# Decay tables of a head pair: VectorE's small operations given to ScalarE, two sums kept on VectorE behind the sum into v

## The reference, cut to what matters

```
idx = jnp.arange(CHUNK, dtype=jnp.float32)
diff = idx[:, None] - idx[None, :]
allowed = diff >= (1.0 if strict else 0.0)
decay_in = jnp.where(allowed[None], jnp.exp(jnp.where(allowed, diff, 0.0)[None] * log_g[:, None, None]), 0.0)
decay_q = jnp.exp((idx + 1.0)[None, :] * log_g[:, None])[None, :, :, None]
decay_k = jnp.exp((CHUNK - 1.0 - idx)[None, :] * log_g[:, None])[None, :, :, None]
...
    scores = jnp.einsum('bhqd,bhkd->bhqk', qc, kc) * decay_in
    inner = jnp.einsum('bhqk,bhke->bhqe', scores, vc)
    cross = jnp.einsum('bhqd,bhde->bhqe', qc * decay_q, state)
```

## Time and profile before

| | |
|---|---|
| median of 3 runs | 2592.87 us (2592.4 to 2595.53) |
| span of the profiled execution | 2588.9 us; the profile gives no device time of its own, so the 4.0 us to the median are what lies around the span |
| PE busy | 2518.4 us of the span (97%) |
| DVE busy | 1859.0 us (72%) |
| ACT busy | 1166.0 us (45%) |
| POOL busy | 1722.0 us (67%) |
| mean granted TensorE clock | 0.993 |
| the four pairs of the first sequence | about 57 to 583 us of the span |
| the four pairs of the second sequence | about 1343 to 1855 us |

### The profile page before, as it was taken

The page is one execution under the profiler, slowest core; times in us unless marked ns, Lnnn a source line. Parts: engine busy times, 40 slices in busy tenths (PEclk is TensorE's granted clock), DMA queues, the critical chain, the costliest instruction groups (busy, mean ns, idle before and its releaser), DMA issues.

```text
span 2588.9 us, 34797 instructions
## 1 busy us (share of the span) xinstructions
PE 2518.4 (97%) x12684; PEld 2104.9 (81%) x12684; DVE 1859.0 (72%) x2230; ACT 1166.0 (45%) x1770; POOL 1722.0 (67%) x1165
## 2 busy tenths in 40 slices
PE   6999999989999999999999999999999999999998
PEld 3888888878778888878888888888877888888886
DVE  4989898977886666765868898988678555556434
ACT  5433333235654554555633333333455554555443
POOL 1677777756287777645656868686655777775545
PEclk9999999999999999999999999999999999999998
DMA  9124242446144445497631514141541323325764
GB/s 330 41 87 132 84 135 84 151 154 216 41 155 159 155 163 176 149 346 232 187 124 41 161 58 160 59 149 47 190 131 41 126 78 122 106 86 194 207 193 146
DMA packets 296008, 362.14 MB, mean 140 GB/s; under 512 B 17312, under 2 KB 178464, under 8 KB 295840
## 3 DMA queue, kind: packets, MB, share of 16 engines
q1 hardware_dynamic: 292960, 349.44, 41.9%
q10 hardware_dynamic: 2880, 10.49, 1.1%
HBM read 284.36 MB, written 75.50 MB: 139 GB/s over the span
## 4 chain that ended last, share of the span: by engine, by line
PE 66%; DVE 15%; POOL 8%; issue 5%; DMA 4%; ACT 3%; SPq 1%; POOLq 0%; DVEq 0%; ACTq 0%
PE ps L1097 27%; PE ps L1263 14%; PE ps L1527 8%; PE ps L1158 5%; POOL f_w L2187 4%; PE ps L1368 3%; PE ps L1478 2%; DVE late_rows L2670 2%; DMA f_ring<-in_w_in 1%; PE ps L1195 1%; POOL f_ring L2195 1%; DVE merged_t L2970 1%; PE ps L1546 1%; DVE bufB L2820 1%; POOL grs L2208 1%
## 5 line engine op out<-in xcount | busy, mean ns | idle before, releaser
L2248 POOL TENSOR_TENSOR f_w<-f_ring,f_w 128x512 fp32r<-128x512 f32 x434 | 595.5, 1378 | 398.4 <-ACT f_w L1832 393.4
L1097 PE MATMUL ps<-hc_hi,f_w 128*128 128x512 f32 x2240 | 690.7, 389 | 3.5 <-ACT u_act L1906 2.9
L2187 POOL TENSOR_TENSOR f_w<-f_ring,f_w 128x512 fp32r<-128x512 f32 x282 | 444.3, 1587 | 235.4 <-ACT f_w L1648 234.7
L1097 PEld LDWEIGHTS ps<-hc_hi,f_w 128*128 128x128 f32 x2240 | 419.9, 188 | 93.4 <-ACT u_act L1906 3.7
L1097 PE MATMUL ps<-hc_lo,f_w 128*128 128x512 f32 x1120 | 435.7, 389 | 0.0
L1263 PE MATMUL ps<-act_ring,f_w 128*128 128x512 f32 x1848 | 421.5, 390 | 3.0 <-DVE act_ring L2565 2.9
L1263 PEld LDWEIGHTS ps<-act_ring,f_w 128*128 128x128 f32 x1848 | 346.6, 188 | 76.9 <-issue 5.2
L1832 ACT ACTIVATE f_w<-f_ring 128x512 fp32r<-128x512 f32 x434 | 269.8, 623 | 252.6 <-POOL f_ring L2258 109.5
L1527 PE MATMUL ps<-hb,f_w 128*128 128x512 f32 x1440 | 347.4, 395 | 0.0
L1648 ACT ACTIVATE f_w<-f_ring 128x512 fp32r<-128x512 f32 x282 | 175.9, 627 | 353.2 <-POOL f_ring L2195 178.6
L1527 PEld LDWEIGHTS ps<-hb,f_w 128*128 128x128 f32 x1440 | 268.3, 188 | 61.3 <-issue 6.7
(11 more groups left out here) (263 smaller groups left out, 4074.3 us busy)
## 6 DMA issues: line engine op xcount, KB each, us to landing
f_ring<-in_w_in SPq DMA_DIRECT2D x176, 256.0 KB, 4.5
f_ring<-in_w_up SPq DMA_DIRECT2D x160, 256.0 KB, 3.4
f_ring<-gated_out SPq DMA_DIRECT2D x154, 256.0 KB, 3.1
late_rows<-in_w_late SPq DMA_DIRECT2D x64, 512.0 KB, 4.0
gated_out<-gated_up SPq DMA_DIRECT2D x44, 512.0 KB, 4.1
f_ring<-down_sums SPq DMA_DIRECT2D x88, 256.0 KB, 3.0
gated_out<-t_gated SPq DMA_DIRECT2D x22, 768.0 KB, 6.2
f_ring<-in_w_down SPq DMA_DIRECT2D x66, 256.0 KB, 3.5
```

The costliest lines, as they stand in the source:

```text
L1097: ins = pe.matmul(ps_row[:, half_of(bank)], a[:, cols], b, start=i in (0, 1, 3) and k == 0 and n == 0, stop=k == KQ - 1 and n == 2, skip_g ...
L2187: pool.tensor_tensor(out[:, 1, :], raw, out[:, 0, :].bitcast(F32), ALU.subtract).then_inc(mix_lo.sem, 1)
L2248: pool.tensor_tensor(piece_slot(q)[:, 1, :], piece_raw(q), piece_slot(q)[:, 0, :].bitcast(F32), ALU.subtract).then_inc(piece_lo.sem, 1)
```

## The change

The whole of `pairS` and the tables is begun by ACT, in a new function `pair_tables`: it copies the two parts of `pairS`, writes the first term of both score tables (a copy with a scale), and makes both query rows with an Exp that takes the scale itself. DVE keeps one operation for each score table, the addition of the second term (`decay_args`), and its place moves behind `qkv_add(1)` (for `pr` 0 behind the first sums of the input pieces). ACT's last Exp (`decays`) covers two blocks in place of four and moves from behind the seventh piece to behind the thirteenth. `pair_tables` waits for the merge of the pair before, since it overwrites `pairS`, and stands behind the sixth piece. For `pr` 0 it stands ahead of the copy of the first input sum (`t_piece_high(pair, 0)`).

```diff
+            def pair_tables(where):
+                _, seq, pr = where
+                if pr:
+                    act.wait_ge(*mg_done.at(pr_before(where), 2))
+                elif seq == 0:
+                    act.wait_ge(table_step, TABLE_STEPS)
+                else:
+                    act.wait_ge(*mg_done.at(("mix", 0, PAIRS - 1), 2))
+                act.activation(pairS[:, 0:T_BUILT], pairT[:, pr, :], ACT.Copy)
+                act.activation(pairS[:, T_BUILT:T_ALL], cst[:, C_POOL + pr * POOL_COLS:C_POOL + (pr + 1) * POOL_COLS],
+                               ACT.Copy).then_inc(pair_set.sem, 1)
+                act.wait_ge(*pair_set.at(where, 1))
+                for h in range(2):
+                    ins = act.activation(dec[:, h, :], cst[:, C_DIFP:C_DIFP + P], ACT.Copy,
+                                         scale=pairS[:, T_LGF + h:T_LGF + h + 1])
+                ins.then_inc(dec_based.sem, 1)
+                place_of = cst[:, C_QUERY:C_QUERY + P]
+                for d, places in enumerate((place_of, place_of[:, ::-1])):
+                    ins = act.activation(dec[:, 2 + d, :], places, ACT.Exp,
+                                         scale=pairS[:, T_LGQ + d:T_LGQ + d + 1])
+                ins.then_inc(dec_done.sem, 1)
...
-                act.wait_ge(*dec_arg.at(where, 6))
-                act.activation(dec[:, :, :], dec[:, :, :], ACT.Exp).then_inc(dec_done.sem, 1)
+                act.wait_ge(*dec_arg.at(where, 2))
+                act.activation(dec[:, 0:2, :], dec[:, 0:2, :], ACT.Exp).then_inc(dec_done.sem, 1)
...
+                        pair_tables(pair)
                         t_piece_high(pair, 0)
                         decays(pair)
...
-                            if q == 6:
+                            if q == 5:
+                                pair_tables(pair)
+                            if q == 12:
                                 decays(pair)
...
-                    dve.tensor_copy(pairS[:, 0:T_BUILT], pairT[:, bass.ds(pr, 1), :].rearrange("p a b -> p (a b)"))
-                    dve.tensor_copy(pairS[:, T_BUILT:T_ALL],
-                                    cst[:, bass.ds(pr * POOL_COLS + C_POOL, POOL_COLS)]).then_inc(pair_set.sem, 1)
...
+                    def decay_args():
+                        for h in range(2):
+                            dve.wait_ge(*dec_based.at(where, 1))
+                            dve.scalar_tensor_tensor(dec[:, h, :], cst[:, C_DIFN:C_DIFN + P], scal(T_LGB + h), dec[:, h, :],
+                                                     ALU.mult, ALU.add).then_inc(dec_arg.sem, 1)
...
                         qkv_add(1)
+                        decay_args()
                         late(1)
```

More of the change, by code:

```diff
@@ L249 @@
 FIXED = 10208
+TABLE_STEPS = 18
 def constants():
@@ L477, in encoder_program @@
         pair_set = tally("pair_set", 0, mix=1)
-        dec_arg = tally("dec_arg", 0, mix=6)
-        dec_done = tally("dec_done", 0, mix=1)
+        dec_based = tally("dec_based", 0, mix=1)
+        dec_arg = tally("dec_arg", 0, mix=2)
+        dec_done = tally("dec_done", 0, mix=2)
         wpool_in = tally("wpool_in", 0, mix=16)
@@ L2626, in _ @@
                 half = slice(h * DK, (h + 1) * DK)
-                for d, sign in enumerate((1.0, -1.0)):
-                    dve.tensor_scalar(pairT[half, :, T_LGQ + d:T_LGQ + d + 1], lg[half, d, :, h:h + 1], sign, None, ALU.mult)
+                for d in range(2):
+                    dve.tensor_scalar(pairT[half, :, T_LGQ + d:T_LGQ + d + 1], lg[half, d, :, h:h + 1], 1.0, None, ALU.mult)
             for d, col in enumerate((T_LGF, T_LGB)):
@@ L2851, in decayed_q @@
                             dve.wait_ge(*qT_done.at(where, 1))
-                            dve.wait_ge(*dec_done.at(where, 1))
+                            dve.wait_ge(*dec_done.at(where, 2))
                         head = slice(h * DK, (h + 1) * DK)
```

12 lines of the change are left out of this document (removed).

## The result

The changed kernel took 2576.01 us in the median of 5 runs (2574.96 to 2578.24), the kernel before beside it 2592.4 us (2589.58 to 2595.53). The ratio is 0.9936, with a 95% interval of 0.9925 to 0.9947: 16.4 us faster. Two later measurements of the same kernel gave ratios of 0.9944 each. The forecast was faster, 2582.7 us with a range of 2580 to 2591.

What follows compares the result with a forecast made beforehand. PE, busy 97% of the span, was taken as the bound, with gains only from its few waits for DVE: 6 x 1.7 = 10.2 us off 2588.9 gives 2578.7, plus 4.0 around it 2582.7 us; range 2580 to 2591.

Steps and rivals of the forecast that it cites:

- the cap: Most an earlier DVE gives back: PE's waits for `v_sb` (6.6 us) and the rotary embedding (5.0 us), 11.6 us.
- the six pairs: Pairs with `pr` 1 to 3, where PE waits for DVE; gain of 1.7 us each, 10.2 us in all.
- the base: Time added around the profiled span to get the total: 4.0 us, from 2578.7 to 2582.7 us.
- The tiles behind the sums: Next DVE row-product tile, 2.10 us before, starts ahead of POOL and may take 1.15 us: 0.95 us off.
- DVE's end: End of the rotary embedding (L2827) in pair 1: 223.8 us in place of 225.52, 1.7 us earlier.
- The sums: Two second-term additions DVE keeps, now behind `qkv_add(1)`: 1.6 us for both, bounds 0.6 and 2.7 us.
- The hold-ups of the rotary half: First half of DVE's rotary embedding meets POOL's five weight pieces: two delays of 1.05 us, 2.1 us.
- the edge: Fewer DVE delays (223.6 or earlier), both PE waits vanish: 11.6 us, 2581.3 us; counted within the forecast's 0.71.
- the port takes it back: POOL delays DVE on the shared port; gain of -0.4 to 0.8 us a pair, 2588 to 2595 us; chance 0.24.
- POOL's piece for PE: POOL's first of five weight pieces, needed by PE at 200.47, done by about 199.9: no cost, 0.5 us cover.
- Pair 0 of the second sequence: ACT's tables delay the first input copy 2.7 us; its copy of v stays 0.7 us ahead of PE: no cost.
- Nothing given back: Everything after the turning of q and k is released by PE or keeps its distance: no loss expected.

Runs made afterwards that it cites:

- e5: The changed kernel with the two kept DVE sums made twice in pairs with `pr` 1 to 3: 2579.55 us, ratio 0.9957.
- e1: The changed kernel without any table work in pairs with `pr` 1 to 3, on ACT and DVE: 2576.46 us, ratio 0.9942.
- e2: The changed kernel with the two kept DVE sums put back at the pair's start, ahead of the row-product tiles: 2577.48 us, ratio 0.9944.

## Why the prediction was wrong in its size

The step that failed is the size of the cap, the most that the two waits could give back; two smaller terms failed with it. The 6.7 us between 2582.7 and 2576.01 come from three terms: 4.2 us from the six pairs (14.4 and not 10.2), 0.3 us from all other places of the span, and 2.2 us from the base.

- **The cap, "1.94 us in one pair" and 11.6 us in all, was mis-sized.** I took the listed idle times as what the waits cost. The right size is the distance of the blocks' starts, and the trace of before had it (200.47, 213.29 and 225.58 stand in the earlier trace rows, the two rows between them below). There a block of 48 matmuls of 128x256 is followed by the next 5.76 us after its own start (200.47 to 206.23), but 7.06 us after it where the listed wait is 1.13 us. Ahead of the turning it is 6.44 us with a listed wait of 0.81, and 5.48 us in after with none. These are 1.30 + 0.96 us, and with the blocks behind each wait, which are 0.09 and 0.06 us longer than in after, 2.41 us a pair. That is the change of distance in the runs. e5 shows the same from the other side, and e1 that there was no more to be had. Six times the 0.47 us between 2.41 and 1.94 is 2.8 of the 4.2 us.
- **The tiles behind the sums ("I take off 0.95 us") were mis-sized, and with them DVE's end.** I put the end at 223.8; it was 222.40. PE was 0.53 us ahead there, so against PE the end came 0.9 us earlier than forecast. The stretch took 22.3 us and not 23.3, from 200.14 and not 200.5. The sums took 1.64 us (1.6 taken). The hold-ups of the rotary half cost 2.1 us as charged, which was partly luck, since they came in other places than I had named (L2842 in the first half, 1.67 us, and L2843 in the second, 1.78 us; each takes 0.68 us where it is short). But both tiles of `late(1)` were short, 1.21 and 1.22 us: from 210.91 to 213.20 they took 2.0 us less than before, where I had taken off 0.95. The first began as POOL's operation ended, the second 0.32 us ahead of POOL's next. So the end came 0.3 us ahead of PE, and the edge ("PE becomes the only bound") was the case. This is the other 1.4 us.
- **The base.** "The 4.0 us around it" came from setting one execution's span against a median. The run of after that was profiled took 2576.01 us for a span of 2574.2, so 1.8 us lie around it, 2.2 us less than the 4.0. For the kernel before, the later runs have 2.0 us around the span in the mean. By that its profiled execution took some 2590.9 us, 2.0 us below the median of 2592.87, and the other 0.2 us were won outside the span.
- **The range.** Its low end rested on the cap of 11.6 us and 1 us of scatter. With 14.4 us and the base of 1.8 us, the case that I called the edge would have given 2588.9 - 14.4 + 1.8 = 2576.3.

The two rows of PE before that the first point needs, between those of the earlier trace rows:

```profile
206.23 5.92 PE L1459 MATMUL ps<-f_w,hb 128*128 128x256 f32 x48
...
219.14 5.63 PE L1478 MATMUL ps<-hb,f_w 128*128 128x512 f32 x24
```

What held:

- PE's waits for `v_sb` and for `rot` were the price, both are gone in all six pairs, and e1 shows that nothing more was to be had there.
- DVE waits for PE ahead of the first sum, 3.50 us ("some 3 us"), and no DMA is waited for.
- *The rival "the port takes it back"* did not occur. Hold-ups are there: L2836 takes 1.24 us and then 2.32 us for the same shape. The Trainium skill (SBUF — State Buffer, "Who interferes with whom") says that a DVE instruction with two SBUF inputs contends with a GpSimd one that reads SBUF, and that the order of issue decides who blocks. The trace agrees. Of the 12 such operations between 200.14 and 222.40, 8 were long, and each of these had started while one of POOL's ran; of the 4 short ones two started in POOL's idle time and two in the last 0.16 us of an operation of POOL's. I had used the rule only for its worst case, with all held up (225.9). Which ones are held is set by who comes first, and that can be read from POOL's rows, but only once they are known for the changed kernel.
- *ACT.* The six operations took 195.81 to 197.45, 1.6 us, the value taken. One of 128x128 takes 0.39 us (I took 0.3), one of 128x256 0.40 us. There was no wait for the merge. The weight copy behind started at 197.88, 0.09 us later than before (0.6 us against PE); it had waited 0.42 us for POOL's sum (L2233, done at 197.78) and not for the tables. PE never waited for it.
- *POOL's piece for PE.* It was done at 199.04, 0.9 us ahead of PE's 199.94; 0.5 us of cover had been forecast. Both row-product tiles were long (2.32 and 2.31 us), as charged.
- *Pair 0 of the second sequence.* The first input copy started 3.49 us behind the start of the weight copy ahead of it, and 0.54 us behind it before, so 2.95 us later (2.7 forecast). ACT's copy of v ended at 1352.48, 0.7 us ahead of PE's start at 1353.18. The table load took 1.28 us, and from the end of the operation ahead of it (1344.44) to the start of the one behind (1345.76) it was 1.3 us. The Trainium skill (ScalarE: Activation LUTs, "Rules for kernel authors") gives about 2.7 us for a whole switch; the measurement decides.
- *"Nothing given back"* held in the balance (0.3 us more was won outside the six pairs), in part by luck: where the granted clock fell differs from profile to profile, and cost 1.6 us at the change of sequence.

Open: why the granted clock falls at the change of sequence in nine profiles and not in three. No run isolates it.

## What to carry to other kernels

The price of a wait is read from the distance between the starts of the blocks around it, against the same distance where there is no wait; PE's listed idle time was 0.17 and 0.15 us short of that here, and nothing was listed for a wait of 0.27 us. Where DVE is late for PE, work ahead of a step that waits for PE anyway can be moved behind it, or to another engine, and the two gains don't add: the cap is what PE waits. Before a step is moved ahead or behind, ask what it waits for (the queue behind it stands too) and what it frees (a load, and all that SP issues behind that load). Where DVE and POOL work at the same time, lay their rows side by side: here the one that started second was held until the first was done, so that moving a step changed the time of the steps around it.

## What the runs showed of the hardware

- Of a DVE operation with two SBUF inputs and a POOL operation that overlap, the second to start was held until the first was done. In after, DVE's of 128x1024 took 2.32 us in place of 1.22 and ended 1.08 to 1.09 us behind POOL's end; POOL's took 2.06 us in place of 1.29 where DVE was first.
- DVE's time for the same eight small operations was 7.86 us with POOL busy all along (six held up), and 2.6 us where POOL then stood idle (one held up). A 128x16 copy took 1.26 or 0.16 us.
- When DVE started 2.9 us later against PE (e2), it ended only 0.2 us later: 1.6 us of work was gone from the stretch, and one operation fewer was held up.
- An ACT operation of 128x128 took 0.39 us, of 128x256 0.40 us, of 128x16 0.21 us and of 128x512 0.63 us, so the cost is nowhere near proportional to the columns.
- Behind 32 matmuls of 128x1 the granted clock was 0.71 over 5 us in after and 1.00 over 4 us in before, for the same instructions: 5.82 us against 4.39 us for 18 matmuls. Nine of twelve profiles show it at this place, with 5.82 to 7.05 us.
